# Seven block products in place of eight in four more products of a two-layer streaming encoder, with one layer's tables gathered beside one chunk

## The reference, cut to what matters

```python
def trunk_layer(x, ...):
    proj = rmsnorm(x, g_mix) @ w_in                 # 1024 wide: u_a, u_b
    y_a = s5_mixer(u_a)       # state space scan, z = gelu(y); out = z * sigmoid(z @ w_glu)
    y_b = pool_mixer(u_b)     # trailing means of 2, 4, 8, 16 tokens, small products
    x = x + concatenate([y_a, y_b]) @ w_out         # [512 + 512] x 1024
    x = x + square(relu(rmsnorm(x, g_ffn) @ w_ff1)) @ w_ff2     # 4096 hidden
    return x
```

## Time and profile before

| What | Value |
| --- | --- |
| Median of 3 runs | 2046.46 us (2045.38 to 2047.51) |
| The profiled execution's own time | 2044.34 us |
| Its span in the trace | 2042.5 us |
| PE busy | 1997.4 us (98%) |
| DVE, ACT, POOL busy | 60%, 33%, 16% |
| Mean granted clock of PE | 0.997 |

### The profile page before, as it was taken

One profiled execution on the slowest core, in us unless ns is written; L12 is line 12 of the kernel. 1 busy time (PEld: TensorE's weight loads), 2 busy tenths in 40 slices (PEclk: granted clock), 3 DMA queues, 4 the chain that ended last, 5 costly groups with the idle time before them and its releaser, 6 DMA issues.

```text
span 2042.5 us, 31840 instructions
## 1 busy us (share of the span) xinstructions
PE 1997.4 (98%) x13416; PEld 1968.8 (96%) x13416; DVE 1218.7 (60%) x1753; ACT 668.9 (33%) x1022; POOL 335.4 (16%) x424
## 2 busy tenths in 40 slices
PE   7999999999999999999999999999999999999997
PEld 7888999999999999999999889999999999999997
DVE  7989467564646465464548735564646546464646
ACT  6233532111124234242332224342423424242322
POOL 2342030001112020110110330220202111020203
PEclk9999999999999999999999999999999999999998
DMA  5546211222225162445243551152525344252512
GB/s 174 151 131 174 73 57 51 87 63 65 74 64 114 47 125 67 94 89 162 91 134 87 151 166 43 32 109 67 114 60 116 72 95 95 70 114 55 122 42 88
DMA packets 123278, 193.34 MB, mean 95 GB/s; under 512 B 13152, under 2 KB 74112, under 8 KB 122752
## 3 DMA queue, kind: packets, MB, share of 16 engines
q1 hardware_dynamic: 88912, 114.45, 19.1%
q0 software_dynamic: 30480, 63.36, 15.1%
q10 hardware_dynamic: 3744, 13.50, 1.7%
HBM read 123.36 MB, written 27.53 MB: 74 GB/s over the span
## 4 chain that ended last, share of the span: by engine, by line
PE 94%; DVE 3%; ACT 1%; issue 1%; DMA 1%; POOL 0%; ACTq 0%; SPq 0%; DVEq 0%; POOLq 0%
PE sums L658 66%; PE sums L773 23%; PE sums L1023 2%; PE sums L897 1%; PE sums L891 1%; PE sums L799 1%; PE sums L746 1%; ACT w_high L1057 0%; DVE pool_s L1498 0%; DMA y_a<-ya_dram 0%; PE sums L714 0%; DVE rms L1527 0%; DMA ya_dram<-u_blocks 0%; DVE rms L2127 0%; DVE x L2133 0%
## 5 line engine op out<-in xcount | busy, mean ns | idle before, releaser
L658 PE MATMUL sums<-h_high,w_high 128*128 128x408 f32 (+1 forms) x1920 | 426.3, 330 | 10.7 <-DVE w_low L1511 10.7
L658 PE MATMUL sums<-h_low,w_high 128*128 128x408 f32 (+1 forms) x1920 | 422.6, 328 | 0.0
L658 PE MATMUL sums<-h_high,w_low 128*128 128x408 f32 (+1 forms) x1920 | 422.2, 328 | 0.0
L658 PEld LDWEIGHTS sums<-h_high,w_high 128*128 128x128 f32 x1920 | 320.6, 188 | 14.7 <-issue 13.3
L658 PEld LDWEIGHTS sums<-h_low,w_high 128*128 128x128 f32 x1920 | 320.2, 188 | 1.0
L658 PEld LDWEIGHTS sums<-h_high,w_low 128*128 128x128 f32 x1920 | 319.8, 188 | 1.0
L1672 DVE TENSOR_TENSOR x<-sums,x 128x544 f32<-128x544 f32 x308 | 219.5, 722 | 142.7 <-PE sums L773 141.5
L773 PE MATMUL sums<-seven_high,w_high 128*128 128x272 f32 x1232 | 255.0, 288 | 0.7 <-issue 0.7
L773 PE MATMUL sums<-seven_high,w_low 128*128 128x272 f32 x1232 | 254.6, 288 | 0.0
L773 PE MATMUL sums<-seven_low,w_high 128*128 128x272 f32 x1232 | 254.1, 288 | 0.0
L1057 ACT ACTIVATE w_high<-w_raw 128x1024 fp32r<-128x1024 f32 x118 | 124.2, 1053 | 324.6 <-PE sums L658 208.9
(11 more groups left out here) (239 smaller groups left out, 2730.1 us busy)
## 6 DMA issues: line engine op xcount, KB each, us to landing
w_raw<-w_blocks SPq DMA_DIRECT2D x120, 512.0 KB, 3.7
w_low<-w_raw POOLq DMA_DIRECT2D x88, 256.0 KB, 3.5
w_low<-w_raw_more POOLq DMA_DIRECT2D x66, 256.0 KB, 3.3
w_raw<-w_blocks SPq DMA_DIRECT2D x88, 128.0 KB, 2.3
w_raw_more<-w_blocks SPq DMA_DIRECT2D x88, 128.0 KB, 2.5
x<-x_t ACTq DMA_DIRECT2D x8, 544.0 KB, 10.9
u_blocks<-ua_dram SPq DMA_DIRECT2D x64, 68.0 KB, 2.7
ya_dram<-u_blocks ACTq DMA_DIRECT2D x8, 544.0 KB, 3.4
```

What stands on the lines that cost most here:

```text
L658: mm = pe.matmul(ps[tile][:, c, 0:(b - a) * J], lhs, xt[:, k, a * J:b * J], start=(first and n == 0), stop=(last and n == 2))
```

## The change

The change has five parts. (1) SEVEN now holds chunks 2 to 7 of layer 0. (2) In both layers the WOA product becomes a unit of seven too, called a gate: its hidden tiles are the four tiles of y_a. (3) Where a unit ends in a norm (both gates, chunk 7 of layer 0: `u.turns`) the squares, `h_high`, `h_low` and POOL's adds are laid between the unit's own instructions, and the pairs of reads are numbered so that tiles 0 to 3 of x are complete by read 13, and tiles 4 to 7 by reads 24, 25, 26 and 27. (4) All of layer 1's tables are made beside chunk 1, the last `kernels` beside chunk 2's first hidden tile. (5) The loads of `rot` and `bt_all` are issued behind the end of chunk 7's unit, ahead of block 2 of layer 1's w_in. The gate's quarters of weights are fetched at the GLU's second block.

```diff
-SEVEN = (tuple(range(3, 7)), tuple(range(7)))
+SEVEN = (tuple(range(2, 8)), tuple(range(7)))
...
+        self.turns = self.gate or cc == NC - 1
...
+GATES = [Unit(l, None) for l in range(LAYERS)]
...
-        PREP_CHUNKS = {1: 0, 2: 2}
+        FF1_TABLES = {0: ("drive", 0), 1: ("carry", 0), 2: ("drive", 1), 3: ("carry", 1)}
+        FF2_TABLES = {1: ("drive", 2), 3: ("carry", 2), 5: ("drive", 3), 6: ("carry", 3)}
+        FF1_TURNED = {1: ("turn", 0), 2: ("kernel", 0), 3: ("turn", 1)}
+        FF2_TURNED = {2: ("kernel", 1), 3: ("turn", 2), 5: ("kernel", 2), 7: ("turn", 3)}
...
-                    if l == 0 and b == ff_block(l, NC - 1, 3):
-                        z = SEVEN_ENDS[0]
+                    if l == 0 and b == BLOCK_ENDS[0] + 1:
                         prepared(sp)
...
+                        unit_over(UNIT_OF[0, NC - 1])
                         sp.dma_start(rot[:, :, :, :, :].rearrange("p h i g j -> p (h i g j)"), rot_dram).then_inc(rot_in, 16)
                         sp.dma_start(bt_all[:, :, :, :], bt_dram).then_inc(bt_in, 16)
...
-                for n in range(2, KD):
-                    half_tile(B_WOA, T_WOA, n, yah, yal)
+                seven_products(GATES[l])
...
+            def seven_hidden(u):
 
                 for j in range(2):
...
+                    hidden_ready(u, 2 * j)
...
+                    operand(u, j, 0)
...
+                    operand(u, j, 1)
                     if j:
                         for n in range(2):
...
+                            minus_high(u, n)
+                            high(u, n)
+                        minus_high(u, 2)
...
+                    hidden_ready(u, 2 * j + 1)
...
+                if u.turns:
+                    turned_high(u, 4)
+                    turned_square(u, 4)
+                    turned_high(u, 5)
+                    turned_square(u, 5)
+                    turned_high(u, 6)
+                    turned_high(u, 7)
+                    turned_square(u, 6)
+                act.wait_ge(seven_done, u.read + 28)
+                split_hi(u.then + 1)
+                if u.turns:
+                    turned_square(u, 7)
...
                     if n == 24:
-                        split_lo(ff_block(l, cc + 1, 0))
-                split_lo(ff_block(l, cc + 1, 1))
+                        split_lo(u.then)
+                    if u.turns and n in (15, 17, 19, 21):
+                        turned_low((n - 15) // 2)
+                    if u.turns and 25 <= n < 27:
+                        turned_low(n - 21)
+                if u.turns:
+                    turned_low(6)
+                    turned_low(7)
+                split_lo(u.then + 1)
...
+            def unit_lows(u):
+
+                for n in range(N_GROUP):
+                    group_low(u, n)
+                    if u.turns and 10 <= n < 13:
+                        add_square(u.phase, n - 9)
+                if u.turns:
+                    for m in range(KA, KD):
+                        add_square(u.phase, m)
```

More of the change, by code:

```diff
@@ L598, in _ @@
                 for b in range(2, B_FF + 2):
-                    if l == 0 and b == B_GLU + 3:
-                        for q in range(1, 4):
-                            turn_y(q)
                     if 4 <= b < 8:
@@ new lines, in turned_square @@
+            def turned_square(u, m):
+                act.wait_ge(seven_read, u.read + 14 * (m // KA) + 10 + m % KA + 1)
+                if m > 2:
+                    act.wait_ge(sq_added, 7 * (u.phase - 1) + m - 2)
+                act.activation(((tr, ts)[m % 2] if m else rms)[:, :], x[:, m, :], ACT.Square).then_inc(sq_made, 1)
+            def seven_hidden(u):
+                for j in range(2):
+                    hidden_ready(u, 2 * j)
+                    if u.first and j == 0:
+                        kernels(1, 3)
+                    operand(u, j, 0)
+                    if j == 0 and not u.gate:
+                        ahead(u.block + 2, u.tile)
+                    operand(u, j, 1)
@@ L1672, in read, with turned_low @@
+                    to = in_parts(x[:, KA * q + 2 * row + pair, h * HALF:(h + 1) * HALF])
                     v.tensor_tensor(to, banks(n), to, ALU.add).then_inc(seven_read, 1)
-                first, second = slice(0, HALF), slice(HALF, T)
+                def turned_low(m):
+                    if u.gate and m == 0:
+                        v.wait_ge(quarter_summed, u.sum + 4)
+                        for i in range(4, 7):
+                            group_drained(v, u.group + i)
+                    low_h(m, 8 * u.phase + m, lp[:, L_FFN:L_FFN + KD] if u.gate else lp[:, L_NEXT:L_NEXT + KD])
@@ L1675, in seven_chunk @@
                 for j in range(2):
-                    relu(2 * j)
+                    even, odd = (ya[:, 2 * j, :], ya[:, 2 * j + 1, :]) if u.gate else (tr[:, :], ts[:, :])
+                    first, second = slice(0, HALF), slice(HALF, T)
+                    hidden(2 * j)
                     if j == 0:
-                        split_lo(ff_block(l, cc, 2))
-                        if z == 0:
+                        if not u.gate:
+                            split_lo(u.block + 2)
+                        if u.first:
```

495 lines of the change are left out of this document (245 added, 250 removed).

## The result

The changed kernel takes 2058.85 us (median of 4, 2057.35 to 2060.61), the kernel before 2046.99 us beside it (median of 4, 2045.38 to 2049.36). The ratio is 1.0058, 95% interval 1.0045 to 1.0070: 11.9 us slower, where 7.9 were forecast.

What follows compares the result with a forecast made beforehand. PE was taken as the bound, busy 1997.4 of 2042.5 us. Terms -23.5 + 21.0 + 3.4 + 7.0 = +7.9 us on the median 2046.46 gave 2054.4 us, range 2044 to 2062.

Steps and rivals of the forecast that it cites:

- main case: The whole sum with waits at gate fronts and turns: 2054.4 us, band 2050.6 to 2058, chance 0.52.
- signs of being wrong: Fronts under 8 us, h_low at 1.34 us beside adds, or over 2 us wait at layer 1's third block or chunk 1.
- Four products of seven: Chunk 2, chunk 7 and two gates each fall from 47.97 to 42.10 us on PE: 23.5 us less.
- Front of the two gates: PE waits 10.5 us before each gate's first product, as DVE and ACT queues run late: 21.0 us, bounds 3.7 to 12 each.
- Low clock behind it: PE's clock falls after each gate's front wait: 3.4 us for two gates, bounds 0 to 6.
- Turns: At units ending in a norm, DVE's h_low and POOL's adds take turns: 2.5 us per gate, 2.0 at chunk 7, together 7.0.
- Loads ahead of the third block: rot and bt_all ahead of layer 1's third w_in block, which still lands by E + 20: cost 0, uncovered 1 to 3 us.
- E + 15.3: E is the unit's end on PE; the next block's split on DVE was to end 15.3 us after it.
- Rival C: More waits: 12 us at each front, low clock twice per gate, ends 9, third block 3: +18.5, 2065 us; chance 0.12.
- A (turns free): Unit ends cost nothing, DVE and POOL overlapping or adds in time: +0.9, 2047.4 us; chance 0.24.
- B (a short front): Gates start sooner, front waits 3.7 us each: 2033.8 us without the ends, 2040.8 with them; chance 0.12.
- D: Seven products don't save in a gate if reads come slower than 1.50 us: 1 us more per gate, inside the main case.

Runs made afterwards that it cites:

- reordering alone: Changed kernel with the gates' queues in another order, second form (third sigmoid and group 2's negation also moved earlier on ScalarE): 2038.58 us, 0.9955.
- small adds: Changed kernel with POOL's adds of the squares at every turn cut to 8 of 1088 columns, making wrong norms: 2054.61 us, 1.0036.
- reordered kernels: Changed kernel with the gates' queues written in another order, same operations: first form 2044.38 us, second form 2038.58 us.
- h_low last: Changed kernel with h_low of x's tiles 4 and 5 moved behind the unit's last read at all three turns: 2062.76 us, 1.0072.

## Why the prediction was right, and by how much it was off

The sum forecast +7.9 us, the range 2044 to 2062 and slower as the likeliest; measured +11.9, so the direction and the range held. The measured 2058.85 lies 0.85 us above the main case's own band (2050.6 to 2058), and one of the prediction's signs of being wrong came true: a wait of over 2 us at layer 1's third block. Step by step, by the starts of PE's stages in the two traces:

| Step | Forecast | In the trace | Shown by |
| --- | --- | --- | --- |
| Four products of seven | -23.5 | chunk 2: -5.7; the others the same before their own losses | the stages |
| Front of the two gates | +21.0 | 10.5 and 10.6 (20.8 by the waits) | reordering alone, with the clock: -21 |
| Low clock behind it | +3.4 | 3.0 and 2.2, of it 0.3 each at the last reads | low clock gone where the wait is 0.46; 2.9 of short losses stay there |
| Turns | +7.0 | 1.9, 1.9 and, at chunk 7, 3.5 (1.0 in the unit, 0.8 behind it, 1.7 at tile 1) | small adds: -4.5, the 1.7 taken over by the late block |
| Loads ahead of the third block | 0, uncovered 1 to 3 | +4.2 (2.56 wait, the rest low clock) | moved behind: -4.7 |
| Tables beside chunk 1 | 0 | chunks 1 and 2 together 0.2 short of a unit's saving | the stages |

**Front.** Walked right, instruction by instruction: 5.20 against 5.14, 14.46 against 14.39, 10.4 against 10.5. The reordered kernels show that it was the order alone: the same instructions without the wait. The prediction said that "the queues leave no other order"; that was true of the queues as written and not of the work. The bound from below, 3.7 us ahead of the first product, was therefore too high: in the reordered kernels that product starts with no wait, because group 0 can also be negated before the third sigmoid. The front is still not free there, since 2.9 us per gate go inside the unit.

**Clock.** The mechanism was right and the size off: 1.7 us was taken from a wait of 4.10 us. Behind 10.4 us the low level lasted about 6 us in one gate and 4 in the other. In the five traces with this front (ten gates) the unit took 43.9 to 45.2 us, so what follows the wait costs 1.8 to 3.1 us and is not one number.

**Turn.** The exclusion was right and is shown (small adds, h_low last). The sum of +7.0 met 7.3, but not by its own steps: the forecast had the split of the block at E + 15.3 and PE waiting at tile 1. In the gates PE waited ahead of tile 0, because the reads of x are themselves queued behind a blocked h_low, and then lost little at tile 1: a layer's tile 1 there came to E + 14.9, near the forecast of E + 15.3, but from a start that was already 1.4 us late. (The prediction's sum that ends at E + 14.2 comes to E + 14.0; the E + 15.3 behind it is right.)

**Loads: the step that failed.** "It should land by E + 20", needed by E + 24 less the split: it landed at E + 18.1, in time by that reckoning, and cost 4.2 us. What I left out is that ACT's queue holds the rounding of this block ahead of the roots of the norm, so that the block is needed not when its own tile is due but ahead of the roots. Its rounding (1.06 us) and a load of ACT's table (1.28) stand between it and them, and the sums were there at 1053.7, E + 16.9; so it was due at about E + 14.6 and came 3.5 us late, which is what the roots were late (4.7 us behind the start of the sums in place of 1.1). A low clock behind the wait added some 1.6 us, a term that the prediction had for the gates alone. Rival C named this wait with 3 us as one of several, but as lateness of the block for its tile, not as a queue. Added to the forecast it gives 2054.4 + 4.2 = 2058.6 against 2058.85; that this closes so well is partly chance, since the clock's 1.8 us more and some smaller losses stand in the spans' 16.2 us as well.

**Rivals.** A (turns free) falls with the small adds and with the long rows. B (a short front) was wrong for this change and is what the reordered kernels make of it: 2038.6 us, where B gave 2033.8 to 2040.8. D is out: from the fourth read to the 23rd the first gate's reads come 1.49 to 1.52 us apart, the pace of the others.

Two losses in the profiled execution look like scatter and not like a part of the change. PE lost 0.9 us later in layer 1, ahead of the last blocks of the scan, behind a wait for u_blocks of 4.4 us in place of 4.1; over all the traces this wait is 3.7 to 4.9. And 1 us went in two parts at layer 0's GLU: it started at 213.3 in place of 212.8 (212.6 to 213.9 over all the traces), and inside it the wait for z_low was 1.0 us in place of 0.4 (0 to 0.5 in the other runs with the same code up to there). What stays open is the 1.6 us that a reordered gate loses without a wait in the trace.

## What to carry to other kernels

A product made cheaper by extra operand work needs a stage ahead of it that is long enough to hide that work: the same unit that is free behind 11.9 us tiles cost 10.5 us behind 6.0 us tiles, until its queues were written for the short stage, with what the first product needs first; then 2.9 us were left. When a transfer is moved ahead of another, look up what stands behind the consumer of the late one in its engine's queue: it is due when that is due. And when an operation is blocked by another engine, moving the blocked ones together can make it worse, since what was running beside them no longer covers.

## What the runs showed of the hardware

Two things were not expected. Behind nearly equal waits (10.38 and 10.42 us) the low clock lasted from 249.2 to about 255.0 in one gate and from 1271.7 to about 1275.6 in the other, and one wait of 2.59 us brought it on too (0.71 and 0.50 in the next two windows of 2 us), while behind the waits of 1.27 us at the gates' ends the clock stayed 1.00. And in the exclusion both sides stretch: four of POOL's adds took 3.0 to 3.4 us against 2.54 alone, while four h_low in a row took 13.35 us, so that each went in turn with one add and neither engine overtook the other. The adds start 3.55 us apart there, a little less than 1.34 and 2.54 together, so that some 0.3 us of a pair overlaps. The Trainium skill, "SBUF — State Buffer", section "Who interferes with whom", says that the pair of ports DVE and GpSimd share is an exclusive lock, and, where it speaks of DVE's 2-port modes, that the engine that comes second blocks fully. These rows bear that out for h_low, which has two inputs in SBUF, but for those 0.3 us, and add that two queues that are both ready take turns.
